# Attention stages of a two-block kernel: the factor in the query copy, negated maxima, a wait moved from the reciprocal to the exponential, one combining operation

## The reference, cut to what matters

```python
# differential attention (first block), blocks of 128 queries
s = jnp.einsum('bqhcd,bkhcd->bhcqk', qblk, k32) * scale
pr = jax.nn.softmax(s, axis=-1)
pd = pr[:, :, 0] - lam * pr[:, :, 1]
return jnp.einsum('bhqk,bkhe->bqhe', pd, v32)
# grouped and rotated attention (second block)
s = jnp.einsum('bqhgd,bshd->bhgqs', qblk, k).astype(jnp.float32) * scale
p = jax.nn.softmax(s, axis=-1).astype(v.dtype)
return jnp.einsum('bhgqs,bshd->bqhgd', p, v)
```

## Time and profile before

| | us |
|---|---|
| median of 3 runs | 3192.8 |
| lowest and highest run | 3184.38, 3198.31 |
| span of the profiled execution, first to last instruction | 3181.1 |
| its seven attention stages, together | 384.2 |

### The profile page before, as it was taken

How to read it: one execution, slowest core, us unless ns; L and a number is a source line. 1 busy time by engine, 2 the same in 40 slices (tenths; PEclk the granted TensorE clock), 3 DMA queues, 4 the chain that set the end, 5 groups by cost and what they waited for, 6 DMA issues and landing times. The chain is left out here.

```text
span 3181.1 us, 42696 instructions
## 1 busy us (share of the span) xinstructions
PE 3001.6 (94%) x16505; PEld 2496.0 (78%) x16505; DVE 2101.7 (66%) x3030; ACT 1289.5 (41%) x2138; POOL 136.9 (4%) x200
## 2 busy tenths in 40 slices
PE   5999889999989999999998999998999999998997
PEld 2577658888779999998887888876757878886766
DVE  5768645746768789887876669545735744774355
ACT  6642334526444444444344323215334224344243
POOL 1000000001010000000001000000010000000000
PEclk9999999999999999999998999999999999999999
DMA  8867224751667777777784546640512644682333
GB/s 269 272 227 270 90 81 140 259 204 35 232 206 259 251 246 258 242 237 271 262 290 155 175 133 201 206 162 14 185 66 100 206 140 139 217 286 73 106 107 138
DMA packets 255577, 589.24 MB, mean 185 GB/s; under 512 B 21977, under 2 KB 30401, under 8 KB 251024
## 3 DMA queue, kind: packets, MB, share of 16 engines
q1 hardware_dynamic: 246336, 546.64, 52.2%
q0 software_dynamic: 8640, 39.22, 3.5%
q10 hardware_dynamic: 400, 0.66, 0.1%
HBM read 571.72 MB, written 14.72 MB: 184 GB/s over the span
## 5 line engine op out<-in xcount | busy, mean ns | idle before, releaser
L2725 DVE TENSOR_TENSOR w_lo<-raw,w_hi 128x1024 fp32r<-128x1024 f32 (+1 forms) x732 | 860.9, 1191 | 395.6 <-ACT w_hi L2704 381.3
L2704 ACT ACTIVATE w_hi<-raw 128x1024 fp32r<-128x1024 f32 (+1 forms) x732 | 741.5, 1032 | 908.1 <-PE bank L2775 514.5
L696 DVE SCALAR_TENSOR_TENSOR acc<-raw,sc_t,acc 128x1024 f32<-128x1024 f32 x480 | 600.9, 1279 | 36.1 <-DMA acc<-in_b_ada 16.1
L2783 PE MATMUL bank<-f_hT_hi,w_hi 128*128 128x256 f32 x1408 | 400.3, 284 | 0.9 <-DVE w_lo L2725 0.9
L2773 PE MATMUL bank<-w_hi,l_hT_hi 128*128 128x512 f32 (+1 forms) x1056 | 391.5, 371 | 8.5 <-DVE w_lo L2725 8.4
L2784 PE MATMUL bank<-f_hT_lo,w_hi 128*128 128x256 f32 x1408 | 399.1, 283 | 0.0
L2785 PE MATMUL bank<-f_hT_hi,w_lo 128*128 128x256 f32 x1408 | 399.1, 283 | 0.0
L2774 PE MATMUL bank<-w_lo,l_hT_hi 128*128 128x512 f32 (+1 forms) x1056 | 388.0, 367 | 0.0
L2775 PE MATMUL bank<-w_hi,l_hT_lo 128*128 128x512 f32 (+1 forms) x1056 | 387.9, 367 | 0.0
L2783 PEld LDWEIGHTS bank<-f_hT_hi,w_hi 128*128 128x128 f32 x1408 | 270.9, 192 | 2.8 <-issue 1.7
L2785 PEld LDWEIGHTS bank<-f_hT_hi,w_lo 128*128 128x128 f32 x1408 | 271.0, 192 | 0.0
(11 more groups left out here) (436 smaller groups left out, 4653.2 us busy)
## 6 DMA issues: line engine op xcount, KB each, us to landing
raw<-in_w_in SPq DMA_DIRECT2D x240, 512.0 KB, 4.9
raw<-in_w_mod SPq DMA_DIRECT2D x192, 512.0 KB, 5.0
raw<-in_w_ada SPq DMA_DIRECT2D x192, 512.0 KB, 4.6
raw<-in_w_up SPq DMA_DIRECT2D x176, 512.0 KB, 4.8
raw<-in_w_out SPq DMA_DIRECT2D x96, 512.0 KB, 5.0
raw<-in_w_down SPq DMA_DIRECT2D x88, 512.0 KB, 5.3
raw<-in_w_in SPq DMA_DIRECT2D x32, 288.0 KB, 3.2
raw<-in_w_ukv SPq DMA_DIRECT2D x16, 512.0 KB, 4.0
```

The lines of the kernel that those rows point to most:

```text
L696: e.scalar_tensor_tensor(acc[a][:, :], raw[s % RAW_SLOTS][:, :], scalar, acc[a][:, :], ALU.mult, ALU.add).then_inc(fma_done, 1)
L2704: e.activation(slot(w_hi[u % SPLIT_SLOTS], g.width), slot(raw[s % RAW_SLOTS], g.width), ACT.Copy).then_inc(hi_ready, 1)
L2725: e.tensor_tensor(slot(w_lo[u % SPLIT_SLOTS], g.width), slot(raw[s % RAW_SLOTS], g.width), slot(w_hi[u % SPLIT_SLOTS], g.width).bitcast(F3 ...
L2783: e.matmul(o, hi[:, kk, c], xh[:, k, 0:n], start=first, stop=False)
```

## The change

The factor (`scale`) is multiplied into the queries as they are copied out of their bank, so the scores come out scaled. The maximum is written negated by the reduction itself, and the operation that negated and scaled it is gone; the exponential has no scale. Two reductions of an item no longer wait for each other. In the stages with one score matrix TensorE's turn waits for the exponential instead of the reciprocal, and VectorE's order becomes query copy, maximum, reciprocal, output. In the differential stage both reciprocals are one instruction over two neighbouring columns, a tiny operation makes minus lambda times the first sum times the second reciprocal, and one operation adds the second exponential, times that, to the first; the first reciprocal is multiplied in at the output. The statistics rotate through four places instead of three, and the output waits for the item's reciprocal or combination.

```diff
--- before.py
+++ after.py
@@ -1046,7 +1046,7 @@
 
             def pe_turn(e, i):
                 gi = ib + i
-                e.wait_ge(a_probs, gi + 1)
+                e.wait_ge(a_exp if C == 1 else a_probs, gi + 1)
                 if i >= lag:
                     e.wait_ge(a_trcopy, gi - lag + 1)
                 for j in range(nk):
@@ -1094,12 +1094,13 @@
                     e.wait_ge(a_tr, gi - 1)
                 for c in range(C):
                     last = e.activation(Pb[:, i % 2, c, 0:keys], sbank(i, c)[:, 0:keys], ACT.Exp,
-                                        bias=stat(i, c, 1), scale=scale, accum_out=stat(i, c, 2))
+                                        bias=stat(i, c, 0), accum_out=stat(i, c, 1))
                 last.then_inc(a_exp, 1)
 
-            def stat(i, c, what):
-                o = 72 + (i % 3) * 12 + c * 6 + what
-                return tiny[:, o:o + 1]
+            def stat(i, c, what, n=1):
+
+                o = 72 + (i % 4) * 4 * C + what * C + c
+                return tiny[:, o:o + n]
 
             def act_trcopy(e, i):
                 gi = ib + i
@@ -1126,48 +1127,42 @@
                 e.wait_ge(a_prep, hb + h + 1)
                 if h >= 2:
                     e.wait_ge(a_scores, ib + (h - 1) * nq)
-                last = e.tensor_copy(qT[:, h % 2, 0:nq * P], q_bank[:, 0:nq * P])
+                last = e.tensor_scalar(qT[:, h % 2, 0:nq * P], q_bank[:, 0:nq * P], scale, None, ALU.mult)
                 if rope is not None:
-                    last = e.tensor_copy(rope[0][:, h % 2, 0:nq * P], q_bank[0:64, nq * P:2 * nq * P])
+                    last = e.tensor_scalar(rope[0][:, h % 2, 0:nq * P], q_bank[0:64, nq * P:2 * nq * P], scale, None, ALU.mult)
                 last.then_inc(a_qcopy, 1)
 
             def dve_max(e, i):
                 e.wait_ge(a_scores, ib + i + 1)
-                if i >= 3:
-
-                    e.wait_ge(a_exp, ib + i - 2)
-                    e.wait_ge(a_out if C == 1 else a_probs, ib + i - 2)
+                if i >= 4:
+
+                    e.wait_ge(a_out, ib + i - 3)
                 for c in range(C):
-                    chain(e, "dve", e.reduce_max(stat(i, c, 0), sbank(i, c)[:, 0:keys], AX_X))
-                for c in range(C):
-                    last = e.tensor_scalar(stat(i, c, 1), stat(i, c, 0), -scale, None, ALU.mult)
+                    last = e.reduce_max(stat(i, c, 0), sbank(i, c)[:, 0:keys], AX_X, negate=True)
                 last.then_inc(a_max, 1)
 
             def dve_probs(e, i):
                 e.wait_ge(a_exp, ib + i + 1)
                 if C == 1:
-                    e.reciprocal(stat(i, 0, 3), stat(i, 0, 2)).then_inc(a_probs, 1)
+                    e.reciprocal(stat(i, 0, 2), stat(i, 0, 1)).then_inc(a_probs, 1)
                     return
-                for c in range(2):
-                    chain(e, "dve", e.reciprocal(stat(i, c, 3), stat(i, c, 2)))
-                chain(e, "dve", e.tensor_tensor(stat(i, 1, 4), stat(i, 1, 3), neg_lam, ALU.mult))
-                chain(e, "dve", e.tensor_scalar(Pb[:, i % 2, 1, 0:keys], Pb[:, i % 2, 1, 0:keys], stat(i, 1, 4), None, ALU.mult))
-                e.scalar_tensor_tensor(Pb[:, i % 2, 0, 0:keys], Pb[:, i % 2, 0, 0:keys], stat(i, 0, 3),
-                                       Pb[:, i % 2, 1, 0:keys], ALU.mult, ALU.add).then_inc(a_probs, 1)
+                chain(e, "dve", e.reciprocal(stat(i, 0, 2, 2), stat(i, 0, 1, 2)))
+                chain(e, "dve", e.scalar_tensor_tensor(stat(i, 0, 3), stat(i, 0, 1), neg_lam, stat(i, 1, 2), ALU.mult, ALU.mult))
+                e.scalar_tensor_tensor(Pb[:, i % 2, 0, 0:keys], Pb[:, i % 2, 1, 0:keys], stat(i, 0, 3),
+                                       Pb[:, i % 2, 0, 0:keys], ALU.mult, ALU.add).then_inc(a_probs, 1)
 
             def dve_out(e, i):
                 h, n = items[i]
                 e.wait_ge(a_pv, ib + i + 1)
+                e.wait_ge(a_probs, ib + i + 1)
                 o = out_of(h, qtiles[n])
                 if gated is not None:
                     if i == 0:
                         e.wait_ge(aux_landed, gated[1])
-                    e.scalar_tensor_tensor(o, banks[products[i % 2]][:, 0:P], stat(i, 0, 3), gated[0](h, qtiles[n]),
+                    e.scalar_tensor_tensor(o, banks[products[i % 2]][:, 0:P], stat(i, 0, 2), gated[0](h, qtiles[n]),
                                            ALU.mult, ALU.mult).then_inc(a_out, 1)
-                elif C == 2:
-                    e.tensor_copy(o, banks[products[i % 2]][:, 0:P]).then_inc(a_out, 1)
                 else:
-                    e.tensor_scalar(o, banks[products[i % 2]][:, 0:P], stat(i, 0, 3), None, ALU.mult).then_inc(a_out, 1)
+                    e.tensor_scalar(o, banks[products[i % 2]][:, 0:P], stat(i, 0, 2), None, ALU.mult).then_inc(a_out, 1)
 
             def dve(e):
                 for s in range(-3, N + 1):
@@ -1175,14 +1170,14 @@
                         dve_qcopy(e, items[s + 3][0])
                     if s in extra:
                         extra[s][2](e, k_bank)
-                    if C == 2 and 0 <= s + 2 < N:
+                    if 0 <= s + 2 < N:
                         dve_max(e, s + 2)
+                    if C == 1 and 0 <= s + 1 < N:
+                        dve_probs(e, s + 1)
                     if 0 <= s - 1 < N:
                         dve_out(e, s - 1)
-                    if 0 <= s + 1 < N:
+                    if C == 2 and 0 <= s + 1 < N:
                         dve_probs(e, s + 1)
-                    if C == 1 and 0 <= s + 2 < N:
-                        dve_max(e, s + 2)
                     for n in range(ahead):
                         if s == N - 2 * (ahead - n) + 1:
                             fill["dve"](e, n)
```

## The result

The changed kernel takes 3147.5 us (median of 4 runs, 3143.85 to 3151.28); the kernel before, timed beside it, 3191.6. The ratio is 0.987, with a 95% interval from 0.986 to 0.989: faster by 1.3%. (The ratio times the 3192.8 of the earlier runs is 3151.9, inside it.) The span of the profiled execution went from 3181.1 to 3145.9 us.

What follows compares the result with a forecast made beforehand. Attention was taken as bound by VectorE's own sum, two-engine loops and waits that idle TensorE some 50 us. Terms summed to 29.8 us: span 3181.1 to 3151, plus 11.7 gives 3163 us; own range 3154 to 3171, with rivals 3149 to 3180.

Steps and rivals of the forecast that it cites:

- What bounds it: Attention stages: TensorE's idle time, some 50 us, caps any gain apart from the clock; rotated stages' steady part cannot gain.
- Differential stage: Differential attention stage: shorter VectorE work brings an item from 3.78 to 3.12 us, saving 10.5 us in all.
- The term for the ends: Differential stage, behind the last maxima: two further passes of output and combination, 0.64 us shorter each, 1.3 us.
- The rival of a loop of 3.45 in every item: VectorE-TensorE handover holds differential items at 3.45 us, bunching halves the rest: gains 14 us, 3179 us; chance 0.12.
- Query copies: Multiplying the factor into the query copies adds 0 to 0.4 us on the differential stage's path; upper end taken.
- Negated reduction: The reduction that writes the negated maximum takes the same 0.69 us as the plain one.
- Inserted pieces: Grouped stages, iterations with inserted transposition pieces: loop from 3.45 to 2.78 us; 5.2 us first layer, 4.0 second.
- Context stage: Grouped stage over the context: maximum first removes TensorE's wait for a late exponential; 4 us of 6.3 idle.
- Turn's wait: Stage ends, turn no longer waiting for the reciprocal: 1.3 us per long rotated, 1.1 short rotated, 1.2 per long grouped.
- Sum to median: The median lies 11.7 us above the profiled span, outside the edited work, so span 3151 becomes 3163 us.
- The clock, chance 0.14: Rival: TensorE, waiting less, keeps 2.4 GHz through most low-clock stretches; 8 us more gain, 3155 us; chance 0.14.
- Slower: Rival: the negated reduction makes a second pass over the columns, costing 40 us against 30 gained: 3203 us; chance 0.03.

Runs made afterwards that it cites:

- the changed kernel's second execution: The changed kernel run once more with no edit: 3147.4 us, ratio 0.988 to the kernel before.
- the doubled reductions: The changed kernel with every reduction done twice (128 more): 3172.2 us, ratio 0.994 to the kernel before.

## Why the prediction was nearly right, step by step

*What bounds it.* Mostly confirmed (that idle time is the bound is not, see the context stage): the four stages with idle time gained, and the rotated kinds kept their steady items of 3.39/4.27 us in every kernel and gained at their ends alone.

*Differential stage, 10.5 forecast, 11.2 measured.* Intervals of 3.46 and 2.78 were worked out; the maxima are 3.45 and 2.85 apart, a pair 6.30 instead of 6.24. The term for the ends was low: 14 intervals at 0.63 to 0.64 make 9.0, which leaves 2.2 for start and end where 1.3 were allowed. The longer interval was worked out from TensorE's scores alone. The rows give two limits that agree to 0.01 us: the scores end at 391.65 + 1.13 = 392.78, and VectorE's own steps, 1.73 to the output, 1.38 through the combination and 0.34 for the query copy, which the prediction left out there, make 3.45. The 3.46 was right, in part by luck. The rival of a loop of 3.45 in every item fell.

*Query copies.* Forecast 0 to 0.4 us, upper end taken; measured 0: the copy with the factor lasts 0.42 us, as the plain one in the earlier trace rows. The rule of the Trainium skill, "VectorE: DVE Perf Modes", section "Why PSUM operands drop a tier", gave this 0, and the trace now agrees with it. For a multiplication by a column it doesn't quite: 128 columns out of a bank take 0.34 to 0.35 us, against 0.29 for the plain copy in the earlier trace rows.

*Negated reduction.* As taken: 0.68. (The 0.25 us for the two negations are 0.28 by the earlier trace rows, 381.39 to 381.67; the sum doesn't use them.)

*Inserted pieces, 2.78 us forecast and measured.* The first layer's grouped stage went from 54.7 to 49.2, 5.5 where 6.4 were forecast. The clock took more than the missing part: 0.90 now against 0.97 in the earlier trace rows, 0.07 x 49.2 = 3.4 us. In the changed kernel's second execution the stage has nearly the clock of before (0.96, with 3.4 us at 1.2 GHz in either) and lasts 46.7, so the edit itself gave 8.0. Of these the iterations with pieces gave 4.7, the end 0.7, and the items ahead of the first piece 2.6, a term that the prediction put at nothing. In the second layer the forecast had 5.2, and 6.1 came: the 4.0 taken of its 7.0 idle us was a guess from above and below, and 5.4 of them went (7.0 to 1.6).

*Context stage, 4.0 forecast, 7.2 measured.* The window went from 31.3 to 24.1 us. This is the term that was mis-sized most. The prediction counted only TensorE's idle time there, 6.3 less 2, and 3.4 of it went. But the stage also had a clock of 0.96 in the earlier trace rows and has 1.00 now, 0.04 x 31.3 = 1.3 us. The remaining 2.5 lie in TensorE's busy time too: 148 matmuls take 21.2 us instead of 25.0. The step from start to start shows why. Ahead of the scores of the earlier trace rows, and at such a place in the changed kernel, where nothing waits:

```profile
2221.96 0.61 PE L1063 MATMUL bank<-l_v,l_gPT 128*128 128x128 f32 x4
```

```profile
2199.66 0.61 PE L1063 MATMUL bank<-l_v,l_gPT 128*128 128x128 f32 x4
2200.11 0.60 PE L1040 MATMUL bank<-l_gkT,l_gqT 128*128 128x256 f32 x2
```

The scores start 0.95 us behind the products in before and 0.45 where nothing waits, so TensorE waited 0.50 us, and the page calls 0.34 of them idle. The other 0.16 are the part by which consecutive records overlap. In before 18 matmuls of this stage start behind a gap, in the changed kernel 5; 13 x 0.16 is an estimate of 2.1 us, most of the 2.5. So part of what the page calls busy was waiting, and the idle time was no upper bound.

*Turn's wait, 3.7 us and parts of two other terms.* The gain at the ends came (3.1 and 1.5 us against 2.4 and 1.3), the cause was named wrong: at the ends of the rotated stages the new order with the old wait brings all of it, and beside it the turn's wait is worth some 0.8 us, at the end of the context stage.

*The pair's edits, one by one.* The first pair lasts 70.2 us in the changed kernel at a clock of 0.98, 72.2 with the negation back, 77.5 with the order back, 78.8 with order and turn back, 84.8 before. The negation is worth 2.0 with the new order. Under the old one 6.0 are left between 78.8 and 84.8, for the negation and the query copies' factor together, so the terms don't simply add; no run takes the two apart there.

*Sum to median.* The prediction added 11.7 us to the span as time "outside the edited work". This step failed. Every execution, of either kernel, lasts 1.7 to 1.9 us longer than its span (3147.73 against 3145.9), so there is no such constant. Of the 15.5 us between forecast and median this step made 10.1 (11.7 instead of 1.6), the terms of the sum 5.1 (a span of 3151 instead of 3145.9). The profiled execution of before was a quick one: 33 further executions of that kernel lie between 3179.9 and 3200.2, with a granted clock of 0.978 in the quickest and 0.970 in the slowest, while the changed kernel's eight lie between 3143.6 and 3151.3, at 0.975 to 0.977. So the 44.1 us between the medians are 35.2 between the spans, and 8.9 by which the profiled execution of before was quicker than its median (8.7) and that of after slower than its own (0.2). Executions with the same granted clock say the same: at 0.976 before takes 3183.9 us on average (four executions) and the changed kernel 3148.4 (three), 35.5 apart; at 0.975 it is 35.0 and at 0.977 37.3. So some 35 to 37 us are the edits, and the rest of the 44 is that before ran at lower clocks in most of its executions.

*The clock, chance 0.14.* Half right. In the two profiled executions the mean clock is the same 0.976, so the 35.2 us are, in sum, not the clock's. Averaged over executions the clock is 0.974 before and 0.976 after; 0.002 of 3180 us are some 6 us of the 44. In the differential stage, where the rival had its largest part, the clock went only from 0.93 over 71.1 us to 0.94 over 59.8, worth 1.4 us. Whether the 6 us are the change's own or would change with any edit is open: the kernels with part of it have averages from 0.9725 to 0.977, in no order that goes by their edits.

*Slower, chance 0.03.* Its trigger didn't occur, and its price was too high: the doubled reductions cost 25 us, not 40.

## What to carry to other kernels

Where two engines hand work back and forth in a closed loop, add up the start-to-start steps of a single turn: if the sum is the measured distance, each edit inside the loop is worth its full time until the other engine's own work is the longer; here the sum of the steps met the measured distance to 0.01 us. Before crediting a removed wait, ask whether another edit of the same change makes the awaited thing early; only undoing each by itself tells. A single profiled execution is one draw from the runs: look at how its time stands to the median before adding the difference as a constant.

## What was not expected of the hardware

Two reductions of 512 columns out of a bank with no wait between them take 1.29 us together, and repeated ones start 0.60 us apart while each lasts 0.68; with a wait between them they take 1.41. The Trainium skill, "VectorE: DVE Perf Modes", section "The DRAIN you can't avoid", found that a semaphore behind each of several copies cost nothing; for these reductions the rows show 0.12 us for one.

A program on one core, whose code in a stretch is unchanged, takes 1713.1 to 1720.6 us for it by how long TensorE is granted 1.2 GHz there (68 to 85 us), and the whole kernel before spreads over 20 us with its granted clock. Stage lengths in the trace, compared at equal clock, resolved what medians could not.
